# A hybrid decoder step: its first projections on unscaled x, the token factor applied later, and a new order of two weight loads

## What is computed

```python
def rmsnorm(x, g):
    xf = x.astype(jnp.float32)
    y = xf * lax.rsqrt(jnp.mean(xf * xf, axis=-1, keepdims=True) + EPS)
    return y.astype(x.dtype) * g
...
    h = rmsnorm(x, norm_mix_g)
    q, kc, vc, ks, vs, kw, vw, gates, glu = project(h, w_in, b_gate)
...
def conformer_conv(glu_in, prev, conv_w, conv_b, ln_g, ln_b):
    a, gate = jnp.split(glu_in, 2, axis=-1)
    u = a * jax.nn.sigmoid(gate)
    ext = jnp.concatenate([prev, u], axis=1)
    y = jax.nn.silu(layernorm(causal_dwconv(ext, conv_w, conv_b), ln_g, ln_b))
```

## Time and profile before

| what | us |
|---|---|
| median of 3 runs | 3529.93 |
| lowest, highest | 3529.3, 3535.41 |
| the profiled execution | 3542.26 |
| its span | 3540.4 |
| TensorE busy in it | 3319.6 (94%) |
| DVE busy | 1572.1 (44%) |
| ACT busy | 364.7 (10%) |

### The profile page before, as it was taken

One profiled execution on the slowest core, in us unless ns is written; L12 is line 12 of the kernel. 1 busy time (PEld: TensorE's weight loads), 2 busy tenths in 40 slices (PEclk: granted clock), 3 DMA queues, 4 the chain that ended last, 5 costly groups with the idle time before them and its releaser, 6 DMA issues.

```text
span 3540.4 us, 41195 instructions
## 1 busy us (share of the span) xinstructions
PE 3319.6 (94%) x14754; PEld 2661.4 (75%) x14754; DVE 1572.1 (44%) x3220; ACT 364.7 (10%) x861; POOL 50.6 (1%) x79
## 2 busy tenths in 40 slices
PE   6999999799987789997989999999999999999997
PEld 4888887577644468856868888888888888888876
DVE  2699011144552133332254454455455445547456
ACT  2000011111341110012100000000000000000003
POOL 0000001100000000000000000000000000000002
PEclk8999999799997899999889999999999999999999
DMA  5222222332004442164122232223223222313212
GB/s 174 60 72 71 74 60 93 100 96 84 1 1 159 128 144 74 49 216 139 48 86 81 65 101 83 71 71 107 75 66 96 83 71 76 102 61 105 76 55 91
DMA packets 309662, 306.91 MB, mean 87 GB/s; under 512 B 12664, under 2 KB 295932, under 8 KB 307759
## 3 DMA queue, kind: packets, MB, share of 16 engines
q1 hardware_dynamic: 302586, 283.01, 25.5%
q0 software_dynamic: 2928, 18.69, 1.5%
q10 hardware_dynamic: 4032, 3.67, 0.4%
HBM read 291.36 MB, written 23.14 MB: 89 GB/s over the span
## 4 chain that ended last, share of the span: by engine, by line
PE 88%; DVE 3%; SPq 3%; DMA 2%; ACT 2%; issue 2%; POOL 0%; DVEq 0%; ACTq 0%; POOLq 0%
PE ps L878 53%; PE ps L847 18%; PE ps L1104 5%; PE ps L842 3%; PE ps L1287 2%; PE ps L871 1%; PE ps L1143 1%; PE ps L1252 1%; SPq L734 1%; SPq L735 1%; PE ps L1374 1%; PE ps L975 0%; PE ps L1131 0%; PE ps L1132 0%; DMA weight_ring<-in_cache_v_win 0%
## 5 line engine op out<-in xcount | busy, mean ns | idle before, releaser
L847 PE MATMUL ps<-xT_region_b,weight_ring 128*128 128x272 f32 x2560 | 588.1, 393 | 1.9 <-DVE region_c L1790 1.1
L847 PEld LDWEIGHTS ps<-xT_region_b,weight_ring 128*128 128x128 f32 x2560 | 486.4, 190 | 102.3 <-ACT v_tok L1513 1.3
L878 PE MATMUL ps<-xT_region_b,weight_ring 128*128 128x272 f32 x2112 | 501.7, 394 | 9.8 <-DVE xT_region_b L2293 9.8
L878 PEld LDWEIGHTS ps<-xT_region_b,weight_ring 128*128 128x128 f32 x2112 | 403.4, 191 | 93.6 <-issue 10.3
L878 PE MATMUL ps<-region_c,weight_ring 128*128 128x272 f32 x1536 | 370.6, 393 | 0.0
L878 PE MATMUL ps<-region_f 128*128 128x272 f32 x1408 | 339.9, 395 | 5.5 <-DVE region_f L1821 5.5
L878 PEld LDWEIGHTS ps<-region_c,weight_ring 128*128 128x128 f32 x1536 | 291.6, 190 | 60.1 <-issue 0.5
L878 PEld LDWEIGHTS ps<-region_f 128*128 128x128 f32 x1408 | 269.4, 191 | 61.8 <-DVE region_f L1821 6.0
L878 PE MATMUL ps<-region_f,weight_ring 128*128 128x272 f32 x1088 | 262.0, 395 | 6.3 <-DVE region_f L1808 4.9
L878 PEld LDWEIGHTS ps<-region_f,weight_ring 128*128 128x128 f32 x1088 | 208.4, 192 | 50.3 <-issue 5.3
L1473 ACT ACTIVATE ext<-ps 128x272 f32<-128x272 f32 x100 | 39.7, 397 | 1660.1 <-PE ps L878 1660.1
(11 more groups left out here) (318 smaller groups left out, 3415.5 us busy)
## 6 DMA issues: line engine op xcount, KB each, us to landing
weight_ring<-in_w_ffn_gate SPq DMA_DIRECT2D x44, 1024.0 KB, 4.9
weight_ring<-in_w_ffn_up SPq DMA_DIRECT2D x44, 1024.0 KB, 4.9
weight_ring<-in_w_in SPq DMA_DIRECT2D x36, 1024.0 KB, 5.2
weight_ring<-in_w_ffn_down SPq DMA_DIRECT2D x64, 512.0 KB, 4.1
weight_ring<-in_w_out SPq DMA_DIRECT2D x16, 1024.0 KB, 5.3
weight_ring<-in_w_ffn_down SPq DMA_DIRECT2D x32, 384.0 KB, 3.6
region_f<-in_cache_k_cmp SPq DMA_DIRECT2D x64, 128.0 KB, 2.0
region_f<-in_cache_v_cmp SPq DMA_DIRECT2D x64, 128.0 KB, 2.0
```

The lines of the kernel that those rows point to most:

```text
L847: mm = pe.matmul(PS[:, 2 * j + h, 0:HALF], lhs(kt), rhs(kt, h), start=(kt == 0), stop=(kt == n - 1))
L878: mm = pe.matmul(prod(k, r), lhs[:, t, :], rhs[:, t, :], start=(t == 0), stop=(t == m - 1))
```

## The change

For the first norm, the gain and the token factor are taken apart.

- ACT (even tiles) and DVE (odd tiles) write HTL = XT x gain, without the token factor. TensorE does tile 0 of group 0 on it, then turns the rows that are not gains, then sums the squares, then does tile 1.
- The squares are added up by DVE over the 16 tiles (SG) while ACT squares; TensorE's share is 2 matmuls instead of 32.
- When the token factor RS is there, DVE multiplies each tile of HTL by it in place, once tile 1 has used it (`s_raw`). Tiles 2 and 3 of the group and all that follows take the scaled tiles. The results of tiles 0 and 1 are multiplied by RS in DVE before the convolution.
- The gate products come behind group 0 instead of ahead of it.
- The turns of x go through all eight banks (`x_bank`); job k waits for job k-8.
- SyncE loads the gain rows on a semaphore of their own (`s_vrow`), then slabs 0 and 1, then the other rows, the gate weights, and slabs 2 and 3. The spill of x to memory waits for the turned x instead of for the normed tiles.
- In the compression stage, SyncE's first two slabs of the value matrix are issued after the pages of step 21 instead of step 19.

The core of the diff:

```diff
...
+        s_vrow = sem("gain_rows_loaded")
+        s_gain = [sem("gained_by_act"), sem("gained_by_dve")]
+        s_xsq = sem("first_squares_ready")
+        s_xad = sem("first_squares_added")
+        s_xss = sem("first_squares_summed")
+        s_raw = sem("raw_tile_used")
+        s_g0 = sem("first_gate_scaled")
...
         FFN_TICKS = OUT_TICKS + sum(7 * n + 32 for n in FFN_CHUNKS)
         NRM, c = {}, 0
-        for k, (name, n) in enumerate((("mix", 16), ("lnmu", 8), ("lnvar", 8), ("gconv", 8), ("gattn", 8),
+        for k, (name, n) in enumerate((("mix", 0), ("lnmu", 8), ("lnvar", 8), ("gconv", 8), ("gattn", 8),
                                        ("mem", 0), ("ffn", 0))):
...
         def bank(k):
             return PS[:, 6 + k % 2, :]
+        def x_bank(k):
+            return PS[:, (k - jobs["x"]) % 8, :]
+
         def x_job(k):
             tt, m = divmod(k - jobs["x"], 4)
             n = P if tt < 4 else SAMP
             return [(XT[:, 4 * m:4 * m + 4, tt * P:tt * P + n],
-                     bank(k).rearrange("p (a t) -> p a t", a=4)[:, :, 0:n])]
+                     x_bank(k).rearrange("p (a t) -> p a t", a=4)[:, :, 0:n])]
...
-                sp.dma_start(VECR[r:r + 1, :], A[n]).then_inc(s_rows, 16)
...
+            def glu_slabs(i, first=0, end=4):
+                for j in range(first, end):
+                    if type(i) is not int:
+                        sp.wait_ge(s_used[j], i + SGR["glu"])
+                    col = i * 256 + (GLU + (j // 2) * P + (j % 2) * CCH)
+                    sp.dma_start(RING[:, j, :].rearrange("p (t n) -> p t n", t=KT),
+                                 w_tiles(w_in)[:, :, ds(col, P)]).then_inc(s_slab[j], 16)
+
+            glu_slabs(0, 0, 2)
             sp.dma_start(CONVR[0:CW, :], A["conv_w"][0]).then_inc(s_rows, 16)
             for r, n in enumerate(("conv_b", "conv_ln_g", "conv_ln_b", "grp_norm_conv_g")):
...
-
...
-            glu_slabs(0)
-            sp.wait_ge(s_h, KT)
+            glu_slabs(0, 2, 4)
+            turned(sp, end_of("x"))
             sp.dma_start(SPILL, XR[:, 0:KT * TOK]).then_inc(s_sp, 16)
             with sp.Fori(1, 4) as i:
                 glu_slabs(i)
...
                 if step == 1:
...
-                if step == 19:
+                if step == 21:
                     w1_slab(1, 0)
                     w1_slab(1, 2)
...
                 src = X4[tt] if tt < 4 else XS
                 for m in range(4):
                     k = jobs["x"] + 4 * tt + m
-                    tr_bank(k)
+                    if k >= 8:
+                        pe.wait_ge(s_te[k % 2], (k - 8) // 2 + 1)
                     for a in range(4):
-                        ins = turn(bank(k)[:, a * P:a * P + n], src[:, (4 * m + a) * P:(4 * m + a + 1) * P])
+                        ins = turn(x_bank(k)[:, a * P:a * P + n], src[:, (4 * m + a) * P:(4 * m + a + 1) * P])
                     ins.then_inc(s_tr, 1)
-            pe.wait_ge(s_rows, 16 * 18)
+            pe.wait_ge(s_vrow, 16 * 7)
...
+            def rows_turned():
+                pe.wait_ge(s_rows, 16 * 11)
+                k = jobs["conv"]
                 tr_bank(k)
...
+            def gate_products():
+                pe.wait_ge(s_wg, 48)
+                pe.wait_ge(s_ps[1], 1)
+                for kt in range(KT):
+                    for h in range(2):
+                        mm = pe.matmul(PS[0:GATES, 2 + h, 0:HALF], WG[:, kt, :], HTL[:, kt, h * HALF:(h + 1) * HALF],
+                                       start=(kt == 0), stop=(kt == KT - 1))
+                mm.then_inc(s_gm, 1)
+
+            def first_group():
+                for j in range(4):
+                    pe.wait_ge(s_slab[j], 16)
+                    if j == 2:
+                        pe.wait_ge(s_rt, 1)
+                    if j == 3:
+                        turned(pe, end_of("cmpp"))
+                    w = RING[:, j, 0:KT * P].rearrange("p (t n) -> p t n", t=KT)
+                    for kt in range(KT):
+                        if j == 0:
+                            pe.wait_ge(s_gain[kt % 2], kt // 2 + 1)
+                        if j == 2:
+                            pe.wait_ge(s_h, kt + 1)
+                        for h in range(2):
+                            mm = pe.matmul(PS[:, 2 * j + h, 0:HALF], w[:, kt, :], HTL[:, kt, h * HALF:(h + 1) * HALF],
+                                           start=(kt == 0), stop=(kt == KT - 1))
+                        if j == 1 and kt < KT - 1:
+                            mm.then_inc(s_raw, 1)
+                    mm.then_inc(s_used[j], 1)
+                    if j == 0:
+                        rows_turned()
+                        pe.wait_ge(s_ones, 1)
+                        pe.wait_ge(s_xad, KT - 1)
+                        for h in range(2):
+                            mm = pe.matmul(PS[:, 4 + h, 0:HALF], ONES[:, :], SG[:, h * HALF:(h + 1) * HALF], start=True, stop=True)
+                        mm.then_inc(s_xss, 1)
+                gate_products()
+
+            def glu_group(i):
+                for j in range(4):
+                    pe.wait_ge(s_slab[j], i * 16 + 16)
+                    pe.wait_ge(s_ps[j], i)
+                    if j == 1:
+                        pe.wait_ge(s_gs, 1)
+                    w = RING[:, j, 0:KT * P].rearrange("p (t n) -> p t n", t=KT)
+                    tile(j, KT, lambda kt: w[:, kt, :], hrhs(HTL)).then_inc(s_used[j], 1)
+
+            first_group()
+            with pe.Fori(1, 4) as i:
+                glu_group(i)
+
...
             turned_tiles("x", x_job)
             turned_tiles("vec", vec_job)
+            act.wait_ge(s_tr, end_of("vec"))
+            turned(act, end_of("vec"))
+            for kt in range(0, KT, 2):
+                act.activation(HTL[:, kt, :], XT[:, kt, :], ACT.Copy, scale=VEC[:, kt, 0:1]).then_inc(s_gain[0], 1)
+            for kt in range(KT):
+                if kt >= 3:
+                    act.wait_ge(s_xad, kt - 2)
+                act.activation(SQ[kt % 2] if kt else SG[:, :], XT[:, kt, :], ACT.Square).then_inc(s_xsq, 1)
             turned_tiles("conv", conv_job)
             turned_tiles("state", state_job)
             turned_tiles("cmpp", cmpp_job)
             act.wait_ge(s_const, 16)
-            turned(act, end_of("x"))
-            squares("mix", lambda kt: XT[:, kt, :], lambda kt: None)
-
+            act.wait_ge(s_xss, 1)
+            act.activation(halves(SG[:, :]), PAIR[2], ACT.Sqrt, bias=cst("eps"), scale=1.0 / D).then_inc(s_rt, 1)
+
+            act.wait_ge(s_g0, 1)
+            act.activation(SG[:, :], SG[:, :], ACT.Sigmoid).then_inc(s_sg, 1)
+            act.wait_ge(s_used[3], 1)
+            act.wait_ge(s_u, 1)
+            act.activation(halves(SG[:, :]), PAIR[3], ACT.Sigmoid).then_inc(s_sg, 1)
             act.wait_ge(s_gm, 1)
             act.wait_ge(s_wg, 48)
             act.activation(halves(GT), PS[0:GATES, 2:4, 0:HALF], ACT.Sigmoid, bias=BG[:, :]).then_inc(s_gs, 1)
-            act.wait_ge(s_rs, 1)
             def glu_gate(i):
                 for t in range(2):
                     act.wait_ge(s_used[2 * t + 1], i + 1)
-                    if t or type(i) is not int:
-                        act.wait_ge(s_u, i * 2 + t)
+                    act.wait_ge(s_u, i * 2 + t)
                     act.activation(halves(SG[:, :]), PAIR[2 * t + 1], ACT.Sigmoid).then_inc(s_sg, 1)
-            steps(act, 4, glu_gate, peel=True)
+            with act.Fori(1, 4) as i:
+                glu_gate(i)
...
             turned_tiles("x", x_job)
-            turned_tiles("vec", vec_job)
+            dve.wait_ge(s_tr, end_of("vec"))
+            turned(dve, end_of("vec"))
+            for kt in range(1, KT, 2):
+                dve.tensor_scalar(HTL[:, kt, :], XT[:, kt, :], VEC[:, kt, 0:1], None, ALU.mult).then_inc(s_gain[1], 1)
+            for kt in range(1, KT):
+                dve.wait_ge(s_xsq, kt + 1)
+                if kt >= 2:
+                    dve.wait_ge(s_xad, kt - 1)
+                dve.tensor_tensor(SG[:, :], SG[:, :], SQ[kt % 2], ALU.add).then_inc(s_xad, 1)
+            dve.wait_ge(s_xad, KT - 1)
+            for t in range(2):
+                own.step(dve.memset(ext_p[t][:, 0:PREV], 0.0))
             turned_tiles("conv", conv_job)
             turned_tiles("state", state_job)
             turned_tiles("cmpp", cmpp_job)
             turned(dve, end_of("cmpp"))
             inverse_root()
-            normed(KT, lambda kt: HTL[:, kt, :], lambda kt: XT[:, kt, :], lambda kt: VEC[:, kt, 0:1])
-
-
-            for t in range(2):
-                own.step(dve.memset(ext_p[t][:, 0:PREV], 0.0))
+            dve.wait_ge(s_gain[0], KT // 2)
+            dve.wait_ge(s_gain[1], KT // 2)
+            for kt in range(KT):
+                if kt < KT - 1:
+                    dve.wait_ge(s_raw, kt + 1)
+                else:
+                    dve.wait_ge(s_used[1], 1)
+                dve.tensor_tensor(HTL[:, kt, :], HTL[:, kt, :], RS[:, :], ALU.mult).then_inc(s_h, 1)
```

(27 more changed lines are left out.)

41 lines of the change are left out of this document (7 added, 34 removed).

## The result

| what | us |
|---|---|
| changed kernel, median of 4 runs | 3476.72 |
| lowest, highest | 3475.85, 3482.51 |
| kernel before, median of 4 runs | 3532.67 |
| ratio, with its 95% interval | 0.9833 [0.9822, 0.9845] |
| profiled execution, changed kernel | 3482.51 |

The change saves 56.0 us of medians; the forecast was 3477 (3468 to 3497), with a sum of 53.2 us saved. In the two profiled executions the difference is 3542.3 - 3482.5 = 59.8 us, more than the sum. The ratio with its interval is worked out from the single runs and is not the quotient of the two medians, which is 0.9842 and lies inside the interval; in microseconds the interval is 54.8 to 62.9. Where the 53.2 came from and what the rest is, are the two questions of what follows.

The account below looks back on a forecast made before the run. TensorE, with 88% of the chain, was taken as the bound. Start 44.0 plus pages 9.2 made 53.2 us, taken off the median 3529.9 to give 3477 us; range 3468 to 3497.

Parts of the forecast that it names:

- first product: Start: x turned by 18.7 us, then gain-row turns, copy and first gain; first product at 21.3, slab 0 already there.
- low clock in the first tile: First tile of the first group: 2.6 us charged for TensorE's low clock, so it ends at 38.6 instead of 36.0.
- adds end: Squares off TensorE: after gains and two squares, 15 adds at 0.785 us end at 39.6, second bound on the next step.
- second group begins: After three more tiles (44.0 us) and the gate products (14.7), the first group's work ends at 102.2 us, formerly 146.2.
- gain of the start: Start through first group and gate products: 44.0 us saved, all of it reaching the projections.
- gain of the pages: Compression stage, step 20's pages: load wait 6.6 us and low clock behind it, 1.1 and 1.5, go; 9.2 us saved.
- Between the tiles: Between first and second tile: TensorE turns the other rows, 4.0 us at most, sum products end at 43.5.
- Rival 1: Start: the rows, now behind two slabs, come late and TensorE stalls; about 3487 us; chance 0.14.
- Rival 2: Compression stage: the page wait moves to step 22 instead of going, only the start is gained; 3486 us; chance 0.12.
- Rival 3: First group and gate products: the clock stays low throughout; slower, 3548 us; chance 0.03.
- Rival 4: Start: DVE or ACT lose unseen time, such as slower in-place multiplies; some 25 us less gain, 3502 us; chance 0.05.
- The convolution: Tile 0's convolution on DVE starts near 63 us instead of 118; DVE still waits for TensorE, so the 44 us stays.

Follow-up runs that it names:

- start_only: Changed kernel with the compression stage's first two value slabs issued after the pages of step 19 again, not 21: median 3490.11 us, ratio to before 0.9866.
- more_banks: Changed kernel with two of the row turns between first and second tile moved to banks 3 and 2: median 3477.91 us, ratio to before 0.9833.
- banks_and_order: Changed kernel with two row turns moved to banks 3 and 2, and gains and squares taken in turns, tile by tile: median 3477.64 us, ratio 0.9828.
- sums_on_pe: Changed kernel with the squares summed by TensorE in 32 products again, instead of added up in DVE: one profiled execution, 3496.2 us.
- scale_triple: Changed kernel with two more unused DVE multiplies of the same size ahead of each in-place multiply by the token factor: one profiled execution, 3491.7 us.

## Why the prediction was right, and where it was off

The forecast's mechanism held in both parts: TensorE's two stops for the norm are gone, and so is the page stop. Its sum, 53.2, is the difference at the end of the compression in the first pair of profiles. That it agrees to a tenth is luck: against the second profile of the kernel before it would be 49.2, and some terms of the sum were off by one to two us and cancelled.

| step | predicted | measured |
|---|---|---|
| first product | 21.3 | 20.6 |
| low clock in the first tile | 2.6 | 1.7 (0.2 to 3.1 in other profiles) |
| first tile ends | 38.6 | 36.9 |
| adds end | 39.6 | 38.4 |
| second tile begins | 43.5 | 43.4 |
| factor ready | 49.9 | 49.4 |
| last tile in place | 61.4 | 59.7 |
| second group begins | 102.2 | 102.6 |
| gain of the start | 44.0 | 43.5 (41.9 against the second profile of before) |
| gain of the pages | 9.2 | 9.1 (8.6) |

- *First product.* The last turn of x ended at 18.0, 0.7 sooner than taken. The product then waited 1.30 us for slab 0, which the prediction had there already; the first gain was ready at nearly the same time (19.66 and one ACT gain of 0.75).
- *Between the tiles.* Here a term was mis-sized, and another made up for it. I charged TensorE its own 4.0 us for the rows, and saw the adds as a bound of its own, but not that DVE's copies of the rows stand behind its adds and that a turn waits for them. Those waits of 1.02 and 0.34 us in the changed kernel, and the clock that fell again behind them, took what the earlier end of the first tile had given: from 36.9 to 43.4 are 6.5 us, with 4.9 predicted.
- *Adds.* They ran at a pitch of 0.83 us, not 0.785: an add waits for the square, the square for the add two before. They began at 26.0, sooner than I had them.
- *Rival 1* did not come: the rows were not waited for. The loads were late (SyncE stood 11.43 us in the issue of the two slabs and 8.72 in a later one), but the first turn of these rows began at 36.94 without idle time ahead. *Rival 2* did not come either; the page turns have no idle ahead. *Rival 3* came in small: the clock fell twice, and was back in the windows from 24 and from 44 us, as the old gate products had shown it for products in a row. *Rival 4's* waits for the factor are absent.
- *The pages* were right in their sum, by the length of that stretch: 9.1 and 8.6 against the two profiles of before.
- *The convolution* of the first tile began at 61.5 us instead of 118, and DVE is not waited for in the groups after; the difference of 43.5 behind the gated-unit groups is the one at the second group, 146.2 - 102.6 = 43.6.
- *The median.* The sum was taken off 3529.9. In the later experiments the kernel before had medians of 3532.7, 3535.4 and 3536.5, with runs from 3529 to 3545: its own uncertainty is several us, more than that of the sum. That 3477 and 3476.7 agree so closely is luck: beside the kernel before, the changed one was 56 to 58 us faster, not 53.2, and the median that the sum was taken off was 3 us below the later one of 3532.7.
- *The chances.* The listed rivals make 0.95 for faster and 0.03 for slower; the prediction sums them to 0.94 and 0.04.

## What to carry to other kernels

A norm ahead of a product stops TensorE twice, for the sum and for the scaling, but only the gain along the summed dimension must be in the operand: the factor per token can follow on the first tiles' results and reach the stored tiles while TensorE uses them. What such a start then gains is set by whichever of its bounds ends last (loads in order of need, sums off TensorE, copies that queue behind the vector engine's new work), so walk each engine's queue, not only TensorE's. And before a surplus of a few us is explained by the change, profile the same program twice and compare it stage by stage.

## What the runs showed of the hardware

- The same program differed by 13.7 us between two profiled executions, in stages in which TensorE often waits: in part by when the granted clock came back (one pair of products at 1.71 instead of 0.86 us), in part by waits that I didn't follow one by one.
- The clock fell after small stops in some executions and not in others. In the changed kernel it was at 1.00 in the window from 18 to 20 us, in which TensorE turned narrow rows, then stopped for 1.30 us, and the next window has 0.55. In start_only the same work with a stop of 1.35 us left it at 1.00. The cost to the first tile was 1.7 us, 0.2 and, in more_banks, banks_and_order and sums_on_pe, 3.1, after stops of 1.27 us. What decides among them isn't shown.
- In scale_triple, seven pieces of four product records, 1.18 us each, with stops of up to 0.97 us between them, kept the clock at 1.00; with the next such stop, at 78.3, it fell (0.59), and was back in the window from 82 (1.00).
- In-place multiplies of 128x544 on DVE came every 0.64 us back to back (16 in 10.25), where the record of each lasts 0.72.
